# Top-k by pair of heads, first inputs and bias table in another order, and tile 0's convolution on VectorE

## The reference

```python
h = rms_norm(x, mix_norm_g)                      # first block
proj = h @ w_in                                  # latents, forget-attention q/k/v, gates
x = x + (attention_outputs * sigmoid(gates)) @ w_out
h2 = rms_norm(x, ffn_norm_g)
scores = q(h2) . sub_keys                        # 8 heads, 2 halves, 128 keys each
s1, i1 = top_k(scores[..., 0], 16); s2, i2 = top_k(scores[..., 1], 16)
experts = 16 best of the 256 sums s1 + s2        # per token and head
a = <h2, u[expert]>; w = softmax(best) * gelu(a)
x = x + sum over 8 * 16 experts of w * v[expert]
for layer in range(2):                           # second block
    proj = x @ w_in_2
    y = [diff_attention, dilated_attention (8 heads), conformer_conv]
    # conformer_conv: GLU -> causal depthwise convolution of 31 taps -> LayerNorm -> swish -> matmul
    x = layer_norm(ALPHA * x + (y * silu(gates)) @ w_out_2)
```

## Time and profile before

| | before |
|---|---|
| median of three runs | 3510.92 us |
| profiled execution | 3506.42 us |
| its span, first to last instruction | 3504.6 us |
| TensorE busy | 2516.0 us (72%) |
| VectorE busy | 1613.0 us (46%) |
| GpSimd busy | 1151.3 us (33%) |
| ScalarE busy | 477.4 us (14%) |
| bytes moved by DMA | 1190.29 MB, mean 340 GB/s |
| mean granted TensorE clock | 0.866 |

### The profile page before, as it was taken

The page is one execution under the profiler, slowest core; times in us unless marked ns, Lnnn a source line. Parts: engine busy times, 40 slices in busy tenths (PEclk is TensorE's granted clock), DMA queues, the critical chain, the costliest instruction groups (busy, mean ns, idle before and its releaser), DMA issues.

```text
span 3504.6 us, 18823 instructions
## 1 busy us (share of the span) xinstructions
PE 2516.0 (72%) x6780; PEld 1202.7 (34%) x6780; DVE 1613.0 (46%) x1820; ACT 477.4 (14%) x1141; POOL 1151.3 (33%) x775
## 2 busy tenths in 40 slices
PE   6999998948696969830172666554566659998997
PEld 3444444424242424410031223221232224444443
DVE  1101111667565656579865556565566641011201
ACT  2221222112020212100000001010100001111111
POOL 0000000044132213335759734348953407101600
PEclk9999999968898998975596787877788879999998
DMA  7787776799999999996997999998899977887775
GB/s 271 258 281 264 269 266 219 275 413 410 422 408 422 410 421 404 413 370 261 422 414 272 374 422 421 422 373 353 325 420 422 422 302 256 279 289 247 250 259 185
DMA packets 164877, 1190.29 MB, mean 340 GB/s; under 512 B 18472, under 2 KB 18728, under 8 KB 20656
## 3 DMA queue, kind: packets, MB, share of 16 engines
q1 hardware_dynamic: 88704, 640.98, 49.0%
q0 software_dynamic: 74192, 539.00, 37.7%
q10 hardware_dynamic: 1888, 9.10, 0.7%
HBM read 1186.92 MB, written 2.10 MB: 339 GB/s over the span
## 4 chain that ended last, share of the span: by engine, by line
PE 36%; DMA 33%; DVE 14%; POOL 12%; ACT 3%; issue 2%; ACTq 0%; DVEq 0%; POOLq 0%
PE psP L1138 24%; DMA rows<-in_peer_u,tk 18%; DMA rows<-in_peer_v,tk 12%; DVE x_sb L356 6%; PE psO L1165 6%; POOL rows L787 5%; POOL work L807 4%; POOL work L806 3%; DVE rows L348 2%; PE psO L1173 2%; DMA ring<-in_w 1%; DMA ring<-in_wq 1%; PE psX L1224 1%; PE psX L1209 1%; PE psX L1247 1%
## 5 line engine op out<-in xcount | busy, mean ns | idle before, releaser
L1138 PE MATMUL psP<-ring,hT 128*128 128x512 f32 x3584 | 1645.8, 614 | 109.4 <-DMA ring<-in_w 88.6
L1138 PEld LDWEIGHTS psP<-ring,hT 128*128 128x128 f32 x3584 | 688.6, 197 | 989.2 <-issue 813.4
L787 POOL DMA_INDIRECT rows<-in_peer_u,tk x256 | 364.5, 1424 | 1268.6 <-DVEq L640 683.1
L348 DVE CUSTOM_DVE_ANT_0 rows<-rows,hrow 128x2048 f32<-128x2048 f32 x256 | 596.9, 2346 | 381.9 <-DMA rows<-in_peer_u,tk 378.8
L356 DVE SCALAR_TENSOR_TENSOR x_sb<-rows,tk,x_sb 128x2048 f32<-128x2048 f32 x256 | 613.3, 2396 | 292.1 <-DMA rows<-in_peer_v,tk 275.7
L787 POOL DMA_INDIRECT rows<-in_peer_v,tk x256 | 411.8, 1609 | 538.9 <-DVE x_sb L356 461.6
L1165 PE MATMUL psO<-ring,work 128*128 128x512 f32 x832 | 382.5, 612 | 2.0 <-DMA ring<-in_w 1.9
L1150 PE MATMUL psX<-kst,x_sb 128*128 128x128 f32 x64 | 15.7, 425 | 301.1 <-DVEq L652 249.1
L1165 PEld LDWEIGHTS psO<-ring,work 128*128 128x128 f32 x832 | 160.1, 198 | 185.9 <-issue 185.2
L807 POOL TENSOR_TENSOR work<-work 128x512 f32<-128x512 f32 x120 | 202.8, 1690 | 9.4
L479 DVE SCALAR_TENSOR_TENSOR work<-psX,small,work 128x128 f32<-128x128 f32 x96 | 27.0, 345 | 317.3 <-PE psX L1247 316.9
(11 more groups left out here) (289 smaller groups left out, 1510.0 us busy)
## 6 DMA issues: line engine op xcount, KB each, us to landing
ring<-in_w SPq DMA_DIRECT2D x572, 1024.0 KB, 6.8
ring<-in_wq SPq DMA_DIRECT2D x32, 1024.0 KB, 6.5
ring<-in_w SPq DMA_DIRECT2D x8, 512.0 KB, 4.2
rows<-in_peer_u,tk POOLq DMA_INDIRECT x256, 18.5
rows<-in_peer_v,tk POOLq DMA_INDIRECT x256, 15.4
x_sb<-in_x SPq DMA_DIRECT2D x2, 1024.0 KB, 6.6
kv<-in_bias_t ACTq DMA_DIRECT2D x1, 1536.0 KB, 12.7
ring<-in_w SPq DMA_DIRECT2D x2, 640.0 KB, 4.1
```

The source lines that it names most:

```text
L348: V.tensor_tensor_reduce(out=rows[:, b, :], in0=rows[:, b, :], in1=hrow[:, t, :], scale=1.0, scalar=0.0, op0=ALU.mult, op1=ALU.add, accum_ ...
L787: pool.indirect_dma_start(out=rows[:, b, :], out_offset=None, in_=a["peer_u" if s < SLOTS else "peer_v"], in_offset=bass.IndirectOffsetOnA ...
L1138: last = MM(psP[:, c % 2, 0:wide], src[:, kk, :], w[:, k, :], start=(kk == 0 and not begun), stop=(kk == 4 * nu - 1))
```

## The change

Four things change. (1) `experts` does the top-k for a pair of heads at a time: one chunk of four rows of scores, its two heads' candidates and expert numbers, and then releases 32 of the 128 gathers of `u`. The scratch memory of this shrinks to one row buffer (tile 0) or 2048 columns of `kv` (tile 1), so the other five row buffers take gathers before tile 0's top-k is done. The slots are dealt out anew: `EMIX` gives 0 + 0 + 3 + 3 + 3 slots inside `experts(0)`, `MIX1` sums to 175, `EMIX[1]` gives 24 before tile 1's top-k and 8 + 8 + 8 + 6 inside it, and `finish_rows(0)` keeps 18. (2) The first transposes wait for two inputs and not for six, and VectorE normalises half of the first `x`. (3) The bias table, its mask rows, the sub-keys and the gain row are loaded at other places. The bias is finished in the middle of the first group and not ahead of it. (4) Tile 0's convolution runs on VectorE, one tap behind each slot from the first group's keys on. Beside these, `c_step` of the first group moves two units further on TensorE.

```diff
+EMIX = [[0, 0, 3, 3, 3], [24, 8, 8, 8, 6]]
-MIX1 = [8, 26, 15, 26, 15, 26, 12, 26, 15, 20]
-GELU1 = 6
+MIX1 = [10, 27, 16, 27, 14, 25, 15, 26, 15]
+GELU1 = 5
+BUF = [n % 5 if n < 15 else (n - 10) % NB for n in range(2 * TT * SLOTS)]
...
+            def conv_tap(l, k):
+                if k == 0:
+                    dve.wait_ge(h_in, l + 1)
...
+                for c in range(CC):
+                    w = col("conv_w", (l * CC + c) * TAPS + k)
...
+                        own.add(V.scalar_tensor_tensor(out=cacc[:, c, :], in0=convh[:, c, k:k + P], scalar=w, in1=cacc[:, c, :],
+                                                       op0=ALU.mult, op1=ALU.add))
+                own.own()
+                if k == TAPS - 1:
+                    dve.sem_inc(conv_dve, 1)
...
                 while peer["n"] < peer["lo"] + round((peer["hi"] - peer["lo"]) * f):
                     slot()
+                    if conv["k"] is not None:
+                        conv_tap(conv["l"], conv["k"])
+                        conv["k"] = conv["k"] + 1 if conv["k"] < TAPS - 1 else None
...
+            def norm_x0():
+                dve.wait_ge(h_norm, 1)
+                for d in (1, 3):
+                    w = slice(512 * d, 512 * (d + 1))
+                    V.tensor_scalar(hrow[:, 0, w], x_sb[:, 0, w], rsx[:, 0:1], None, ALU.mult).then_inc(h_norm2, 1)
...
+                for i in range(4):
+                    stage(EMIX[t][1 + i])
+                    mix(0.3)
+                    seen["sc"] += 1
+                    dve.wait_ge(sc_done, seen["sc"])
+                    link(V.tensor_copy(sc, v3(psO[:, i, :], NK)))
                     dve.sem_inc(sc_taken, 1)
+                    top16([(sc[:, j, :], vals[:, j, :], idx3[:, j, :]) for j in range(4)])
+                    mix(0.6)
...
+                    top16([(cand[:, 256 * h:256 * (h + 1)], best[:, 16 * h:16 * (h + 1)], posu[:, 16 * h:16 * (h + 1)])
+                           for h in range(2)])
...
+                    dve.sem_inc(ids_ready, 1)
+                    if i < 3:
+                        mix(1.0)
...
+                    if t == 0 and l == 0 and g == 0:
+                        mix(0.5)
+                        dve.wait_ge(bias_in, 32)
...
                     take_kT(kind, t, i, l)
+                    if t == 0 and g == 0:
+                        conv.update(k=0, l=l)
...
             def gather(n):
...
-                if s == 0:
-                    pool.wait_ge(ids_ready, t + 1)
+                if s < SLOTS and s % 32 == 0:
+                    pool.wait_ge(ids_ready, 4 * t + s // 32 + 1)
+                if n == 15:
+                    pool.wait_ge(ids_ready, 4)
...
-            for n in range(2 * SLOTS, 4 * SLOTS):
-                gather(n)
-                for l in range(LAYERS2):
-                    k = n - (h_mark[l] + NB)
-                    if 0 <= k < TAPS:
-                        tap(l, 0, k)
...
             def startup():
+                for dst, name in ((kst[:, :], "konst"), (cols[:, :], "cols")):
+                    act.dma_start(dst, a[name]).then_inc(k_in, 16)
...
-                act.wait_ge(in_in, 16 * N_IN)
                 act.wait_ge(x_in, 16)
                 norm_x(0)
...
+                act.dma_start(skT, a["sub_keys"]).then_inc(sk_in, 16)
                 if t == 0:
                     act.wait_ge(x1_in, 16)
                 else:
-                    keys_and_gain(1)
+                    gain_row(1)
+                    act.dma_start(bias2, a["bias_t"]).then_inc(bias_in, 16)
+                    act.dma_start(lnc, a["log_count"]).then_inc(bias_in, 16)
...
-                    units(begin2("q", g), 0, 4, 4, hT)
+                    c = begin2("q", g)
+                    units(c, 0, 2, 4, hT)
+                    if g == 1:
+                        c_step(t, r)
+                    units(c, 2, 4, 4, hT)
```

More of the change, by code:

```diff
@@ L607, in experts @@
-                for half in range(2):
-                    for i in (2 * half, 2 * half + 1):
-                        seen["sc"] += 1
-                        dve.wait_ge(sc_done, seen["sc"])
-                        own.add(V.tensor_copy(sc[:, 4 * i:4 * i + 4, :], v3(psO[:, i, :], NK)))
-                    own.own()
-                    dve.sem_inc(sc_taken, 1)
-                    if half == 0:
-                        mix(1.0)
-                        stage(24 if t else 0)
-                    top16([(sc[:, 8 * half + j, :], vals3[:, 8 * half + j, :], idx3[:, 8 * half + j, :]) for j in range(8)],
-                          0.05 + 0.3 * half)
@@ L670, in layer2 @@
                     take_xT(split, "ln")
-                if t == 0 and l == 0:
-                    dve.wait_ge(bias_in, 32)
-                    own.add(V.tensor_tensor(bias2[:, 0:4, :], bias2[:, 0:4, :], over(lnc[:, 0, :], 4), ALU.add))
-                    link(V.tensor_tensor(bias2[:, 4:12, :], bias2[:, 4:12, :], over(lnc[:, 1, :], 8), ALU.add))
                 mix(0.3)
@@ L804, in tap @@
+                if not second:
+                    own.link(T(cacc if k == 0 else csq, moved, wk_, ALU.mult))
+                elif k == 0:
                     own.link(T(cacc, cacc, rep(bias4, P), ALU.add))
                 else:
-                    own.link(T(csq, moved, wk, ALU.mult))
                     own.link(T(cacc, cacc, csq, ALU.add))
-                if k == TAPS - 1:
+                if step == 2 * TAPS - 1:
                     pool.sem_inc(conv_done, 1)
-            for n in range(2 * SLOTS):
+            for n in range(4 * SLOTS):
@@ L812, in _ @@
                 gather(n)
[L813 to L818 removed]
             for l in range(LAYERS2):
[L820 to L821 removed]
+                for step in range(2 * TAPS):
+                    conv(l, 1, step)
                 if l == 0:
```

176 lines of the change are left out of this document (89 added, 87 removed).

## The result

The changed kernel takes **3403.52 us** (median of four runs, 3401.84 to 3407.36), and the kernel before, run beside it, 3508.59 (four runs, 3501.92 to 3516.05). The ratio is 0.970, with a 95% interval of 0.968 to 0.972. The forecast was 3406, in a range of 3355 to 3455. The profiled execution took 3404.22 us with a span of 3402.4, TensorE at 2487.1 us (73%), VectorE 1665.3 (49%), GpSimd 874.5 (26%) and a mean granted clock of 0.881.

What follows compares the result with a forecast made beforehand. TensorE was taken to bound the first and last 700 us, DMA gathers and weights the middle, with GpSimd pacing some stretches; -9 + 8 - 24 + 2 - 68 - 11 = -102 gave 3404.4 or 3408.9, stated as 3406, range 3355 to 3455.

Steps and rivals of the forecast that it cites:

- 76 - 12 + 4 = 68: Tile 0's convolution: 76 us of lost DMA time removed, 6 us per layer for taps, 4 from moved loads; -68 in all.
- the 12 for taps on the path: Tile 0's layers: 6 us per layer allowed for VectorE's taps in places where weights don't flow.
- Rival A: Layer-two stretches: the loss was VectorE's, not GpSimd's, so half of the 76 us comes back; 3460 us, chance 0.13.
- rival C: Convolution: a tap instruction on VectorE costs 1.009 us, as beside GpSimd, so the kernel gets slower; 3541 us, chance 0.04.
- turning point of 0.87 us: Convolution: tap instruction time from which a slot with a tap takes about 5.9 us and eats the other 35 us of gain.
- Rival D: Whole kernel: no change, as the slot order makes TensorE wait elsewhere for just what is gained; 3505 us, chance 0.04.
- The 4 for the moved loads: Tile 0's layers: loads moved elsewhere give back 4 us, counted within the convolution's -68.
- 8 - 24 + 2 - 4 = -18: Tile 0's top-k and slots +8, tile 1's top-k stage -24, earlier bias table load +2, moved loads 4 gained.
- Ten slots end at about 725: Tile 0's top-k: ten slots after the last list end at about 725, where eight ended at 727; TensorE -2 us.
- the first 24 run beside 16 units of weights, 34 x 2.485: Tile 1's stage, slots before top-k: 40 transfers less 6 ready rows, 85 us, and 3 for the normalising.
- The stage's own sign: Tile 1's top-k stage: the transposes of `layer2(0, 0)` come at about 1716 and not 1742.
- Rival B: It gives more: first slots find rows ready and tile 1's top-k hides beside weights; about 3355 us, chance 0.11.

## Why the prediction came out right

**The convolution.** Right in mechanism: GpSimd had set the pace, and the lost transfer time came back nearly whole. My sum was 76 - 12 + 4 = 68. Of these the 76 held, but the 12 for taps on the path were too many: leaving them out gives 4. So 72, as the run with the convolution alone shows. A tap instruction took 283 to 345 ns where I took 0.33. Rival A is excluded by the run that undoes it, rival C by this duration (its turning point of 0.87 us should read 0.90: (5.96 - 2.35) / 4). Rival D, another wait in place of each gain, doesn't fit: nothing of the gains was taken back. The 4 for the moved loads were 6.0 to 7.2. One thing in the mechanism stays open: of the 5.4 us per step, a gather's issue, a multiply and an add take only some 3.7 when no slot holds them up (0.98 + 1.05 + 1.26 and the gaps). The rest is waiting beside slots, and no run separates the two parts.

**The start and `c_step`.** The start gave 10.7 where I took 9: the table load no longer stood behind `x` (it began at 4.73), so the square began at 7.36 and not at 8.7, and `cols` cost 1.18. `c_step` gave 14.5, where I counted two waits, 11; the step that was short is that a wait costs only its own length. The slower granted clock behind it costs 1.9 us more in each layer.

**The top-k.** Here the forecast was too good, and the others' surplus hid it. I had summed top-k, slots, bias table and moved loads to 8 - 24 + 2 - 4 = -18; they gave 10.6 to 12.7. Two steps were off. "Ten slots end at about 725": TensorE came 2 to 3 us later, counted from its first transposes, and not 2 sooner. With the 10.7 us of the start taken off, I had the last list at 689 and the end of the slots at 714. They came at 686.8 and 718.3: eight slots stood ahead of the list and eleven behind it, where I had nine and ten, and VectorE waited 4.9 us for rows in the eleven. And "the first 24 run beside 16 units of weights, 34 x 2.485": they took 103 us and not 88. I had counted the transfers that the stage needs, as though none were for later. The trace moves 42.67 MB in these 103 us, 40.7 units' worth, at 415 GB/s: the ring fetches four units of `layer2(0, 0)` in this time, and GpSimd posts 25 gathers, so the buffers that I had taken off as ready are filled again at its end. That is 15 us. Behind it the stage took 182 us where I had 187, a pair 36.4 (35 forecast). Of the loss at 1550 to 1700 I had said that it wouldn't go away; it grew from 43 to 64 us. The stage's own sign failed with it: the transposes of `layer2(0, 0)` came at 1733.2 and not at 1716, and those of tile 1's layers 87.7 us sooner and not 95. Rival B's thought, top-k beside weights, was worth 21.5 us, but in another deal of the slots than this change has.

**The sum** met the result within 2.5 us by luck, because the errors had both signs: +4 in the stretch up to `forget_sums`, +3.8 in `layer1(1)` (+1 by the means over all traces), +7.6 in `experts(1)`, against -1.7, -10.4 and -3.5 in the others. The 10.4 are the 8.4 for taps and 2.0 that the loads' new places gave beyond the 4 forecast. Taken singly the four undone parts cost 12.2, 67.6, 14.7 and 12.7 us, 107.2 in all, against 105.1 for the whole: the edits add up, each in its own stretch. The sign that would have spoken against it, transfers under 350 GB/s in tile 0's layers, shows in no slice of the page there (377 at the least), though in one stretch of 50 us, over the change of layers (345 at 2233 to 2283).

## What to carry to other kernels

Ask which engine posts the transfers: with arithmetic in the same in-order queue, the transfers go at that queue's pace wherever nothing else fills them, and here it gave back 76 us and cost 4 to move the work to an engine with some 20 of 50 us free. An engine's free time is worth something only where it lies: count the waits beside full transfers, and put the work into these (21.5 us by five numbers), until the inputs of that work come too late. When adding up what a stretch must transfer, add what buffers fetch ahead for the next. And when a sum of several terms comes out right, look at each term by itself.

## What the runs showed of the hardware that I had not expected

**Beside back-to-back slots, GpSimd posts one gather per slot and no more.** That an issue waits for a slot was in the earlier trace rows; that it caps the rate was not. GpSimd's issues in the changed kernel, first beside back-to-back slots, then with VectorE idle:

```profile
1458.97 2.15 POOL L816 DMA_INDIRECT rows<-in_peer_v,tk  x1 [0.30 <-issue]
...
1482.92 0.94 POOL L816 DMA_INDIRECT rows<-in_peer_v,tk  x1 [4.03 <-DVE x_sb L355]
```

The same instruction takes 0.94 us alone and 2.15 beside a chain of slots (2.45 us apart), with 0.30 between. So a stretch bound by slots can't fill its buffers faster than it empties them. This is not what holds the rate at 225 to 269 GB/s while VectorE does top-k and slots alone (1550 to 1700). There GpSimd stands idle for 6.66 and for 11.48 us in each pair until a slot gives a buffer back:

```profile
1559.99 3.00 POOL L816 DMA_INDIRECT rows<-in_peer_v,tk  x1 [6.66 <-DVE x_sb L355]
```

Eight slots in each 36.4 us give back eight buffers of 1 MiB, which is 230 GB/s.

**The other way round** a slot beside GpSimd's taps grows too. In the kernel before, first a multiply that waits for a slot, then a slot that waits for a multiply, and an add that waits for this slot:

```profile
1853.43 2.29 DVE L348 CUSTOM_DVE_ANT_0 rows<-rows,hrow 128x2048 f32<-128x2048 f32 x1 [2.67 <-DMA rows<-in_peer_u,tk]
1854.27 2.36 POOL L806 TENSOR_TENSOR work<-work,cols 128x512 f32<-128x512 f32 x1
...
1870.76 3.72 DVE L348 CUSTOM_DVE_ANT_0 rows<-rows,hrow 128x2048 f32<-128x2048 f32 x1 [3.00 <-DMA rows<-in_peer_u,tk]
1871.27 1.05 POOL L806 TENSOR_TENSOR work<-work,cols 128x512 f32<-128x512 f32 x1
1872.40 3.20 POOL L807 TENSOR_TENSOR work<-work 128x512 f32<-128x512 f32 x1
```

The multiply of 1854.27 ends 0.91 after its slot; the slot of 1870.76 ends 2.16 after the multiply, about its usual length; and the add ends 1.12 after the slot. In the run with the convolution back on GpSimd the longest slot took 3.85 us, where its median was 2.29. By the Trainium skill ("SBUF — State Buffer", the section "SBUF: two separate sides") one of the two holds the shared pair of ports and the other waits. The traces agree in both directions.

**A wait of 5.5 us on TensorE costs 7.3.** The mean granted clock was 0.86 of full speed (2.4 GHz) over the 24 us around it, and 1.00 without it. It was at the lower level, 0.50 or 1.2 GHz, in the transposes behind the wait (2964 to 2966), and back at full speed by 2970; TensorE had stood idle before it fell and worked without a gap before it rose. The three kernels that have the wait take 645.1 to 645.8 us for tile 1's layers, the others with all of the work 628.8 to 630.8.
